# One decoder step: query weights kept uncomposed, transposed queries made per block, ten weight chunks of tile 1 held in the row ring

## The reference, cut to what matters

```python
def peer_block(xt, peer_w_q, peer_sub_keys, peer_u, peer_v):      # xt: 128 tokens x 1024
    t = xt.shape[0]
    q = (xt @ peer_w_q).reshape(t, PEER_HEADS, 2, PEER_D_HALF)      # 1024 -> 2048 = 16 x 128
    s = jnp.einsum('thcd,hcnd->thcn', q, peer_sub_keys)             # 16 products with 128x128 keys
    sv, si = lax.top_k(s, PEER_TOPK)
    ...
    best, sel = lax.top_k(cand..., PEER_TOPK)                       # 16 of 256 pairs, in each head
    gates = jax.nn.softmax(best, axis=-1)
    h = jnp.einsum('thkd,td->thk', peer_u[idx], xt)                 # a gathered row per pick
    a = jax.nn.gelu(h, approximate=False) * gates
    return jnp.einsum('thk,thkd->td', a, peer_v[idx])
```

## Time and profile before

| | |
|---|---|
| time, median of 3 runs | 2993.72 us |
| lowest and highest | 2992.31 and 2998.58 us |
| the profiled execution: span | 2992.2 us |
| PE busy | 2231.6 us (75%) |
| DVE busy | 2016.7 us (67%) |
| ACT and POOL busy | 1041.1 (35%) and 1197.0 us (40%) |
| bytes moved by DMA | 1214.13 MB, mean 406 GB/s |

### The profile page before, as it was taken

The page is one execution under the profiler, slowest core; times in us unless marked ns, Lnnn a source line. Parts: engine busy times, 40 slices in busy tenths (PEclk is TensorE's granted clock), DMA queues, the critical chain, the costliest instruction groups (busy, mean ns, idle before and its releaser), DMA issues.

```text
span 2992.2 us, 29116 instructions
## 1 busy us (share of the span) xinstructions
PE 2231.6 (75%) x8812; PEld 941.4 (31%) x8812; DVE 2016.7 (67%) x4923; ACT 1041.1 (35%) x3233; POOL 1197.0 (40%) x1052
## 2 busy tenths in 40 slices
PE   8989879885798868777685567756786578667565
PEld 6666524552245522222221132212221132111111
DVE  2663457765577655878468865887568765886875
ACT  3232422334233343334333353334333353233222
POOL 0023344434343343444344444444444444444443
PEclk9999989998899989977798789978897789889776
DMA  8599999999999999999999999999999999999998
GB/s 330 204 391 415 403 420 421 418 418 423 420 417 413 413 419 421 416 420 374 424 421 420 413 419 420 410 419 416 417 418 419 408 406 421 420 414 400 418 421 352
DMA packets 195838, 1214.13 MB, mean 406 GB/s; under 512 B 25600, under 2 KB 44872, under 8 KB 62432
## 3 DMA queue, kind: packets, MB, share of 16 engines
q0 software_dynamic: 148608, 1082.20, 87.6%
q1 hardware_dynamic: 47072, 130.07, 11.2%
HBM read 1192.48 MB, written 20.23 MB: 405 GB/s over the span
## 4 chain that ended last, share of the span: by engine, by line
DMA 39%; PE 30%; DVE 16%; issue 7%; ACT 4%; POOL 3%; SPq 1%; POOLq 0%; DVEq 0%; ACTq 0%
DMA ring<-in_peer_uv,idxg 37%; PE ps L1018 14%; DVE ring L1801 8%; PE ps L980 5%; PE ps L700 5%; POOL ring L624 3%; ACT ring L1080 2%; PE ps L961 1%; DMA wo<-in_w_in 1%; DVE columns L1702 1%; DVE columns L1708 1%; DVE columns L1651 1%; PE ps L673 1%; PE ps L717 1%; DVE columns L1712 1%
## 5 line engine op out<-in xcount | busy, mean ns | idle before, releaser
L624 POOL DMA_INDIRECT ring<-in_peer_uv,idxg x1024 | 1181.0, 1153 | 1605.7 <-PE ps L1018 1365.4
L1018 PE MATMUL ps<-ring 128*64 128x512 f32 x4096 | 1231.8, 732 | 677.6 <-ACT ring L1080 675.4
L1801 DVE SCALAR_TENSOR_TENSOR ring<-ring,xlo 128x1024 f32<-128x1024 f32 x512 | 627.0, 1225 | 447.6 <-DMA ring<-in_peer_uv,idxg 397.7
L1801 DVE SCALAR_TENSOR_TENSOR ring<-ring,xhi 128x1024 f32<-128x1024 f32 x512 | 626.6, 1224 | 353.1 <-DMA ring<-in_peer_uv,idxg 343.1
L1018 PEld LDWEIGHTS ps<-ring 128*64 128x64 f32 x4096 | 286.2, 156 | 1455.7 <-ACT ring L1080 1005.4
L1290 ACT ACTIVATE small<-small 128x2 f32<-128x2 f32 x512 | 105.0, 205 | 1692.0 <-DVE ring L1801 1671.6
L1080 ACT ACTIVATE ring<-gdiag,small 128x64 f32<-128x64 f32 x1024 | 302.2, 342 | 16.6
L700 PE MATMUL ps<-wo 128*128 128x176 f32 x1728 | 286.5, 321 | 24.6 <-issue 8.8
L1080 ACT ACTIVATE gdiag<-fold,gateg 128x64 f32<-128x64 f32 x1024 | 294.6, 335 | 1.5
L700 PEld LDWEIGHTS ps<-wo 128*128 128x128 f32 x1728 | 264.7, 194 | 86.5 <-issue 73.9
L980 PE MATMUL ps<-keyw,work 128*128 128x512 f32 (+1 forms) x576 | 275.9, 614 | 0.9 <-ACT keyw L1080 0.7
(11 more groups left out here) (212 smaller groups left out, 1514.0 us busy)
## 6 DMA issues: line engine op xcount, KB each, us to landing
wo<-in_w_in SPq DMA_DIRECT2D x44, 704.0 KB
ring<-in_peer_uv,idxg POOLq DMA_INDIRECT x1024
wo<-in_w_out SPq DMA_DIRECT2D x4, 4096.0 KB, 16.9
ring<-in_w_in SPq DMA_DIRECT2D x7, 1408.0 KB, 7.3
ring<-in_wqT SPq DMA_DIRECT2D x16, 512.0 KB, 4.3
columns<-proj_scratch SPq DMA_DIRECT2D x7, 896.0 KB
proj_scratch<-wo SPq DMA_DIRECT2D x70, 88.0 KB
h<-in_x_prompt SPq DMA_DIRECT2D x9, 512.0 KB, 8.6
```

What stands on the lines that cost most here:

```text
L624: nc.gpsimd.indirect_dma_start(row[r], None, A["peer_uv"], bass.IndirectOffsetOnAxis(ap=experts, axis=0)).then_inc(ld_row[r], 16)
L1018: mm = nc.tensor.matmul(acc[side * HP:(side + 1) * HP, n * 512:(n + 1) * 512], row_u[r][:, 0:HP], row_v[r][:, n * 512:(n + 1) * 512], star ...
L1801: ins = stt(row_u[r], row_u[r], 1.0, (xlo, xhi)[unit % 2][:], ALU.mult, ALU.mult, accum_out=dot[:, r:r + 1])
```

## The change

The query weights stay as they are: `w_q` comes in four loads of 2 MB into `wq`, which stays resident (64 KB of each partition), as do the sub-keys (`skT`, 8 KB). `keyw`, `key_weights` and the 32 copies go. For each block PE makes the queries transposed, 16 chunks of 8 matmuls of 128x128 (`queries`), ACT copies them group by group from PSUM to SBUF (`q_home`, four copies of 128x512), and PE multiplies them with the keys, 16 matmuls of 128x128 (`scores`). `QUERY_STEPS` gives the due tick of each. The top-k starts two ticks later (`TOPK_AT`).

`AHEAD` grows from 8 to 10. Chunks 0 to 4 of tile 1 lie in the lower half of the ring and 5 to 9 in the upper, one DMA for each half; three more (10 to 12) are loaded into `wo` before the loop. POOL fetches units 0 to 3 after piece 4, and units 4 to 7 after piece 9. The stages are 6, not 8, and the descriptor scratch of the gathers is 2048 bytes of a partition, not 8192.

```diff
-STG = 8
+STG = 6
-AHEAD = 8
-RESTING = (3, 4, 5, 6)
-TURNS = [l for l in range(2 * LCH) if l not in RESTING]
+LOWER, UPPER = range(0, 5), range(5, 10)
+AHEAD = len(LOWER) + len(UPPER)
+TURNS = list(range(AHEAD, 2 * LCH))
...
-        return 1 + (q - AHEAD) * 13 // 16 if q < 24 else 14 + (q - 24) * 31 // 24
+        return 1 + (q - AHEAD) * 44 // (EARLY - AHEAD)
...
-            hold(pool, keyw_mm, 2 * NHC)
-            hold(pool, o_mm, 2)
+            hold(pool, pj_mm, NCH + len(LOWER))
+            hold(pool, counted, TILES)
...
                         if b == 0 and unit == RING // 2:
-                            hold(pool, pj_mm, NCH + LAST_OF[RESTING[-1]] + 1)
-                            hold(pool, counted, TILES)
+                            hold(pool, pj_mm, NCH + AHEAD)
...
+            def queries(b, rows, n, c):
...
+                for k in range(KC):
+                    mm = nc.tensor.matmul(F[n][:, c * P:c * P + rows], wq[:, n, k, c * P:(c + 1) * P],
+                                          xT[:, k * P:k * P + rows], start=(k == 0), stop=(k == KC - 1))
+                if c == QG - 1:
+                    mm.then_inc(q_mm, 1)
+
+            def scores(b, rows, n):
...
+                pe.wait_ge(q_out, b * QG + n + 1)
+                for c in range(QG):
+                    mm = nc.tensor.matmul(F[n][0:rows, c * P:(c + 1) * P], q_home[n % 2][:, c * P:c * P + rows],
+                                          skT[:, n * QW + c * P:n * QW + (c + 1) * P], start=True, stop=True)
+                mm.then_inc(sc_mm, 1)
...
+QUERY_STEPS = [(0, 0, 19), (0, 1, 20), (0, 2, 21), (0, 3, 22), (1, 0, 23), (1, 1, 24), (0, QG, 25), (1, 2, 25), (1, 3, 26),
+               (2, 0, 27), (1, QG, 29), (2, 1, 29), (2, 2, 31), (2, 3, 33), (3, 0, 35), (2, QG, 37), (3, 1, 37),
+               (3, 2, 39), (3, 3, 41), (3, QG, 45)]
+QUERY_COPIES = (24, 28, 36, 44)
+SCORE_COPIES = (32, 48)
...
-TOPK_AT = 31
+TOPK_AT = 33
...
-    nc = _bacc.Bacc("TRN2", target_bir_lowering=False, num_devices=1, dynamic_dma_scratch_size=8192)
+    nc = _bacc.Bacc("TRN2", target_bir_lowering=False, num_devices=1, dynamic_dma_scratch_size=2048)
```

More of the change, by code:

```diff
@@ L181, in build @@
         F = [ps[:, 2 + i, :] for i in range(6)]
+        q_home = [proj[:, D + i * QW:D + (i + 1) * QW] for i in range(2)]
         SA, SB = F[5], F[4]
@@ L230, in build @@
         wbuf = [part(KC * CW) for _ in range(2)]
[L231 to L234, removed]
         wbuf.append(ring[:, RING // 2 * ROWW:RING // 2 * ROWW + KC * CW])
-        x_spare = [part(D) for _ in range(2)]
+        x_spare, w_ring = [], []
+        for slots, chunks in ((ring[:, 0:RING // 2 * ROWW], LOWER), (ring[:, RING // 2 * ROWW:], UPPER)):
+            part = space(slots)
+            w_ring += [part(KC * LW) for _ in chunks]
+            x_spare.append(part(D))
+        w_lower = ring[:, 0:len(LOWER) * KC * LW]
+        w_upper = ring[:, RING // 2 * ROWW:RING // 2 * ROWW + len(UPPER) * KC * LW]
+        mask0 = stage[:].rearrange("p a b c d -> p (a b c d)")
         wo_first = by_k(ring[:, RING // 2 * ROWW:RING * ROWW])
@@ L249, in build @@
         xT_late = part(4 * D + KC * SPAD)
-        stg_late = [part(LW) for _ in range(STG - 3)] + stg_wide
+        stg_late = [part(LW) for _ in range(5)] + stg_wide
         w_late = [part(KC * LW) for _ in range(2)]
@@ L301, in build @@
         ld_g1, ld_xT_first, ld_xT_early = sem("ld_g1"), sem("ld_xT_first"), sem("ld_xT_early")
-        ld_wq = [sem(f"ld_wq{i}") for i in range(4)]
+        ld_wq = [sem(f"ld_wq{i}") for i in range(QG)]
         ld_x = [sem(f"ld_x{i}") for i in range(5)]
@@ L972, in picking @@
                 t.then_inc(x2T_mm, 1)
-                for n, (begin, pace) in enumerate(((19, 1), (23, 1), (27, 2), (35, 2))):
-                    yield at + begin
-                    if n == 0:
-                        pe.wait_ge(x2T_out, b + 1)
-                    if b == 0:
-                        pe.wait_ge(keyw_out, 8 * (n + 1) + 2)
-                    for k in range(KC):
-                        mm = nc.tensor.matmul(F[n][0:rows, :], xT[:, k * P:k * P + rows],
-                                              keyw[:, k, n * 512:(n + 1) * 512],
-                                              start=(k == 0), stop=(k == KC - 1))
-                        if k % 2 and k < KC - 1:
-                            yield at + begin + (k // 2 + 1) * pace
-                    mm.then_inc(sc_mm, 1)
+                for n, c, tick in QUERY_STEPS:
+                    yield at + tick
+                    if c < QG:
+                        queries(b, rows, n, c)
+                    else:
+                        scores(b, rows, n)
                 if rows == P:
-                    yield at + 44
+                    yield at + 48
                     pe.wait_ge(sc_out, b * 2 + 1)
@@ L1115, in late_pieces @@
                     late_out(q)
-            def key_weights():
-                for n in range(NHC):
-                    for half in range(2):
-                        act.wait_ge(keyw_mm, 2 * n + half + 1)
-                        copy(keyw[:, half * 4:half * 4 + 4, n * NK:(n + 1) * NK],
-                             acc[:, half * 512:(half + 1) * 512].rearrange("p (k n) -> p k n", k=4)
-                             ).then_inc(keyw_out, 1)
-                        yield key_copy_tick(2 * n + half + 1)
             def sample():
@@ L1380, in _ @@
             tell(used, RING)
-            tell(keyw_out, 2)
             sample_roots = Steps(v, sm["root_out"])
```

142 lines of the change are left out of this document (67 added, 75 removed).

## The result

The changed kernel takes **3031.18 us** (median of 4 runs, 3027.54 to 3033.32), the kernel before in the same comparison 2993.87 us (4 runs): ratio 1.0123, 95% interval 1.0111 to 1.0136. The prediction was 2986 us, faster; it is 37 us slower. The profiled execution has a span of 3029.8 us.

What follows compares the result with a forecast made beforehand. From the first gather on, DMA was taken to bound the kernel (bytes divided by rate). Lead -9.9 and loop +2 made -7.9 us: span 2992.2 to 2984, plus 1.5 for the median, 2986 us; range 2978 to 3003.

Steps and rivals of the forecast that it cites:

- Bytes: Before the gathers: 6 more chunks loaded early, 4.33 MB, 10.4 us of the saturated phase; some 44.5 MB in 150 us.
- The start: Chain through block 0 to the first gather: sum +1.4 us, gather at 153.2 us; ends -2.0 and +3.0.
- the term of the clock: PE idling before and after the output projection lowers its clock: +3.4 us, ends 0 and about 5.
- The margin at piece 4: POOL's new wait before the first gathers: piece 4 is stored before the picks are due, with 1 us to spare.
- the gain is given back by a later start: Rival: margin at piece 4 fails, first gather +7 us, 2993 us; chance 0.22.
- Lead: Bytes moved by 160 us: 47.2 MB against 43.1, a lead of 4.1 MB or 9.9 us.
- The loop: Scoring in the loop's blocks: PE's extra 6.9 us a block mostly hidden under saturated DMA; +2 us, ends -5 and +10.
- The samples' bound: Sample block's scores with 8 moving columns: bounded by +6.9 and -20 us, given nothing since PE is half idle.
- PE becomes the bound in the loop: Rival: in three blocks' scoring stretches PE falls behind the rows on their way; 3005 us, all seven blocks 3032; chance 0.12.
- The scratch: Gathers' descriptor ring of 2048 bytes holds 14 gathers, at most 8 unfinished: no cost; rival that POOL waits, 3060, chance 0.03.

Runs made afterwards that it cites:

- the run with fillers: Changed kernel with 11 groups of four unread 128x128 matmuls in PE's gaps before block 0's queries: 3025.39 us, ratio 1.0094.
- SP's order: Changed kernel with SP's move of the second half's picks 7 ticks later in its queue, blocks 1 to 7: 3019.18 us, ratio 1.0085.
- second half earlier: Changed kernel with the second half's top-k 24 ticks behind the first half's, not 26, in blocks 1 to 8: 3015.59 us, ratio 1.0068.
- residual: Changed kernel with the samples' residual loaded ahead of SP's move of the last block's second picks: 3022.25 us, ratio 1.0087.
- column groups: Changed kernel with the samples' 8 token columns as weights, w_q moving, partial products in four column groups of PE: 3019.07 us, ratio 1.0084.
- all five: Changed kernel with SP's order, second half earlier, residual, column groups and fillers together: 2987.96 us, ratio 0.9980 to the kernel before.

## Why the prediction was wrong, point by point

- **Bytes: right.** 297 GB/s over 150 us are 44.6 MB (44.5 were expected), and the DMA is then empty.
- **The start: the term of the clock was mis-sized.** The steps without it were right or a little too dear: with PE's gaps filled, the output projection begins at 73.72 (74.0 was said) and the first gather comes 3.4 us before the old one, where these terms gave -2.0. The clock was put at 3.4 us, with 5 as its upper end, from one row of 3.68 us. It is 9.4 us, by the run with fillers. The half clock came before the output projection too (the matmuls of the sliding window from 62.6, 0.63 us for what takes 0.39, and the transposes; the projection begins 3.1 us later), then in the projection (+2.9), the next transposes (+0.9) and the first queries (+2.5, 13.45 against 10.98 us). Four places, not two, and they stand in one chain, which is 9.4 us longer at the first scores (114.58 against 105.17).
- **The margin at piece 4 held.** The stores' issue ended at 153.2, the picks went at 154.16, and POOL waited for the picks. The rival "the gain is given back by a later start" is right in that the start came later (6.0 us) and in part of the reason (the low clock), but not in the wait, and its 2993 us is 38 us short: a later start is not what made the kernel slower.
- **Lead: 2.0 MB at 160 us, not 4.1** (44.6 + 0.5 against 43.1): 4.7 us and not 9.9. The first gather came 4.7 us later than the 153.2 of the forecast, which is nearly all of the difference.
- **The loop: the step that failed**, +2 us with ends of -5 and +10, where the result shows some 40 (a lead of 4 us at 190 us and 37 us behind at the end). The prediction looked for the price in PE's work under the DMA and found cover for that rightly (a quarter less of queries changes nothing once the rest is mended). It had three edits at nothing that were not: `TOPK_AT` (10 us on the old kernel), the stages from 8 to 6 (4 us alone, 17 us in two holes together with the tick), and the samples' scores, given nothing "since its PE is half idle" (12 us when they were mended, and 8.9 for the residual behind the picks). The samples' bound went from +6.9 to -20 and held PE's time at the full clock alone. For that it was right: 128 and 16 narrow matmuls are 35.4 us, the old 32 were 30.1, +5.3. But as the clock was granted PE took 41.1 us there instead of 29.5, and ACT waited 12.3 us for it. The tick was named ("DVE's top-k has a tick less after ACT's copy") but not followed on SP's queue: behind SP's wait for the picks stand the stores and the samples' residual. The old trace could have told it: SP already stood there for 11 us, and DVE already waited 5.6 us for the residual.
- **"PE becomes the bound in the loop"**, 0.12: in the loop of whole blocks only in block 0, and there it takes a lead away, it does not make the kernel slower than before. The sample block, which that rival left out, is where PE had no idle time and the DMA lost most.
- **The scratch**: nothing, as said; POOL's issues kept 0.94 us. The prediction's estimate from the Trainium skill, DMA: Bandwidth & Descriptors, "The descriptor swizzle" and "Terms", was room for 14 gathers with at most 8 unfinished; the old kernel with 2048 bytes has the same time (ratio 0.9994), which agrees with it. No run shows where the room would end.

The single edits on the changed kernel gain 12.0 (SP's order), 15.6 (second half earlier), 8.9 (residual), 12.1 (column groups) and 5.8 us (fillers): 54 us, and all five together 43. They overlap, since the first two close the same holes and the second and third shorten the same wait. With four runs for each, the order among the five isn't settled.

## What to carry to other kernels

- When a change moves a step that some queue waits for, write down what stands behind that wait in the queue and how many buffers its producer has left. Two small edits to the same slack (later by 6 us, two buffers less) cost 2 to 3 us each in a place, and 9 together.
- Look in the old trace for waits that cost nothing yet, and ask what would lengthen them. Here a wait of 5.6 us for the residual was free and one of 8.4 us was paid in full; waits for a store of about 6 us cost 2 to 3 us, those of 8 us about 8.
- Work that "only fills gaps" can carry the clock of what follows it. Before it is removed, price every matmul in the chain behind it at the half clock, not one.
- Bytes moved out of a stretch help only if DMA bounds it. In block 0, once PE set the pace, most of what they had bought was lost again.

## What the runs showed of the hardware

- A float32 matmul with 8 moving columns takes 0.24 us (1.95 us for 8), like one with 128 columns; the product turned round (8 columns as weights, 512 moving) takes 0.94 us alone and 0.26 us each when four go to four column groups (1.04 us for the four).
- PE can be without idle time and still be granted the lower clock. From 2740 to 2780 us of the kernel with fillers it is busy for 40 of 40 us with these narrow matmuls between pairs, after a stretch with idle time, at a clock of 0.63; the old kernel, with 512 moving columns in the same work, has 30.00 of 30 us busy from 2720 to 2750 and a clock of 1.00. The narrow matmuls alone don't explain it: from 2785 to 2810 the changed kernel has the same mix at 0.98.
- Useless matmuls can shorten a chain: 11 us of them, in PE's gaps, kept the clock at 1.00 and brought the first gather 9.4 us forward.
- A store of 88 KB issued into the saturated DMA frees its stage only after some 13 us (644.69 to 657.8; the median of all such stores, from issue to landing, is 12.7), and the wait for it can be a hole for engines that have nothing to do with it.
